# Low parts first in every second pair of pieces, in the gates, the convolution's output and the block's output projection

## What is computed

```
h = h + (p[i] @ pl_w_up[i]) * jax.nn.sigmoid(h @ pl_w_gate[i])           # plgate

proj = hn @ w_in
u, gb_in, gc_in, v_in, ga_lin, gbr_lin = jnp.split(proj, splits, axis=-1)
y_b = (gb_in * causal_depthwise_conv(gc_in * v_in, conv_w)) @ conv_out_w  # cout
gates = jax.nn.sigmoid(jnp.concatenate([ga_lin, gbr_lin], axis=-1) + b_gate)   # ga, gbr
g_a, g_b = jnp.split(gates, 2, axis=-1)
h = h + (g_a * y_a + g_b * y_b) @ w_o                                     # wo
```

## Time and profile before

| what | value |
|---|---|
| median of 3 runs | 2665.52 us (2665.11 to 2665.89) |
| the profiled execution | 2665.68 us |
| its span, first to last instruction | 2663.6 us |
| mean granted TensorE clock | 0.999 |
| PE busy | 2652.8 us, 15711 matmuls |
| DVE busy | 1658.5 us, 62% |
| ACT busy | 1236.0 us, 46% |
| DMA | 502.92 MB, mean 189 GB/s |

### The profile page before, as it was taken

The page is one execution under the profiler, slowest core; times in us unless marked ns, Lnnn a source line. Parts: engine busy times, 40 slices in busy tenths (PEclk is TensorE's granted clock), DMA queues, the critical chain, the costliest instruction groups (busy, mean ns, idle before and its releaser), DMA issues.

```text
span 2663.6 us, 39872 instructions
## 1 busy us (share of the span) xinstructions
PE 2652.8 (100%) x15711; PEld 2347.5 (88%) x15711; DVE 1658.5 (62%) x1645; ACT 1236.0 (46%) x1355; POOL 0.8 (0%) x7
## 2 busy tenths in 40 slices
PE   9999999999999999999999999999999999999998
PEld 8889888888888888888999999888888888888887
DVE  6567766555565556795676666556765645564555
ACT  5456554444444444565443443444554434443444
POOL 0000000000000000000000000000000000000000
PEclk9999999999999999999999999999999999999999
DMA  8554555655656555555555555555565555565553
GB/s 291 184 174 145 195 189 193 193 193 188 198 181 205 181 199 189 185 191 191 176 175 189 181 184 182 190 182 190 189 205 189 189 189 189 189 198 192 180 192 138
DMA packets 254251, 502.92 MB, mean 189 GB/s; under 512 B 8130, under 2 KB 11652, under 8 KB 253988
## 3 DMA queue, kind: packets, MB, share of 16 engines
q1 hardware_dynamic: 252180, 497.61, 56.6%
q10 hardware_dynamic: 1952, 3.68, 0.4%
HBM read 498.37 MB, written 2.88 MB: 188 GB/s over the span
## 4 chain that ended last, share of the span: by engine, by line
PE 99%; DVE 0%; ACT 0%; DMA 0%; issue 0%; ACTq 0%; DVEq 0%
PE ps L1359 49%; PE ps L1373 24%; PE ps L1392 4%; PE ps L1394 4%; PE ps L1393 4%; PE ps L1412 4%; PE ps L1411 4%; PE ps L1410 3%; PE ps L1403 0%; PE ps L1402 0%; PE ps L1404 0%; PE ps L1322 0%; DMA xtok<-in_x_dram 0%; PE ps L1547 0%; PE ps L1545 0%; PE ps L1546 0%
## 5 line engine op out<-in xcount | busy, mean ns | idle before, releaser
L825 DVE TENSOR_TENSOR lo<-raw,hi 128x1024 fp32r<-128x1024 f32 x940 | 1127.8, 1223 | 852.2 <-ACT hi L491 843.6
L491 ACT ACTIVATE hi<-raw 128x1024 fp32r<-128x1024 f32 x940 | 971.5, 1055 | 1061.2 <-PE ps L1373 483.6
L1359 PE MATMUL ps<-A,hi 128*128 128x512 f32 x3648 | 862.8, 393 | 0.0
L1359 PEld LDWEIGHTS ps<-A,hi 128*128 128x128 f32 x3648 | 675.6, 188 | 140.4
L1359 PE MATMUL ps<-B,hi 128*128 128x512 f32 x1984 | 477.5, 394 | 0.0
L1373 PEld LDWEIGHTS ps<-A,lo 128*128 128x128 f32 x3648 | 438.0, 188 | 12.0
L1373 PE MATMUL ps<-A,lo 128*128 128x256 f32 x3648 | 439.9, 277 | 0.0
L1359 PEld LDWEIGHTS ps<-B,hi 128*128 128x128 f32 x1984 | 365.3, 188 | 74.8
L1373 PEld LDWEIGHTS ps<-B,lo 128*128 128x128 f32 x1984 | 246.1, 188 | 10.0
L1373 PE MATMUL ps<-B,lo 128*128 128x256 f32 x1984 | 247.8, 279 | 0.0
L1412 PE MATMUL ps<-B,lo 128*128 128x258 f32 (+1 forms) x768 | 219.4, 286 | 0.0
(11 more groups left out here) (240 smaller groups left out, 1342.6 us busy)
## 6 DMA issues: line engine op xcount, KB each, us to landing
raw<-in_w_in_dram SPq DMA_DIRECT2D x136, 1024.0 KB, 5.1
raw<-in_ffn_w_dram SPq DMA_DIRECT2D x132, 1024.0 KB, 5.1
raw<-in_w_gate_up_dram SPq DMA_DIRECT2D x88, 1024.0 KB, 5.0
raw<-in_w_down_dram SPq DMA_DIRECT2D x44, 1024.0 KB, 5.1
raw<-in_w_out_dram SPq DMA_DIRECT2D x16, 1024.0 KB, 5.2
raw<-in_pl_w_gate_dram SPq DMA_DIRECT2D x16, 1024.0 KB, 5.1
raw<-in_conv_out_w_dram SPq DMA_DIRECT2D x16, 1024.0 KB, 5.1
raw<-in_w_o_dram SPq DMA_DIRECT2D x16, 1024.0 KB, 5.1
```

The source lines that it names most:

```text
L491: act.activation(hi[:, slot % RING], raw[:, raw_slot, 2 * (slot % 2):2 * (slot % 2) + 2, :], ACT.Copy).then_inc(hi_ready, 1)
L825: dve.tensor_tensor(lo[:, slot % RING], raw[:, slot // 2 % RAWS, 2 * (slot % 2):2 * (slot % 2) + 2, :], hi[:, slot % RING], ALU.subtract). ...
L1359: last = pe.matmul(ps[:, b0 + m, :], high(slot, kk, m), both, start=j == 0 and kk == 0, stop=ends and j == seg.pieces - 1 and kk == 1)
```

## The change

Five segments are added to the set: plgate, ga, gbr, cout and wo, all of two turns with two groups of eight pieces. What is computed stays the same but for the order in which products are added.

```
-SNAKED = {"qk", "out"} | {f"f{i}_{part}{c}" for i in (1, 2) for part in ("up", "down") for c in range(3)}
+SNAKED = {"qk", "out", "plgate", "ga", "gbr", "cout", "wo"} | {f"f{i}_{part}{c}" for i in (1, 2) for part in ("up", "down") for c in range(3)}
```

## The result

The changed kernel takes 2669.23 us (median of 18 runs, 2666.32 to 2670.94) against 2665.43 us (18 runs of the kernel before, 2665.07 to 2666.12). The ratio is 1.0013, 95% interval 1.0007 to 1.0019: slower by 3.8 us, forecast 4.2, and too little to be called a change at the 0.2% that I set. The changed kernel's runs lie 4.6 us apart, those before 1.1; that turns out to have a cause of its own. The profiled execution took 2668.11 us.

What follows compares the result with a forecast made beforehand. TensorE bounds the kernel at 99% of the chain, so only matmul pace and new waits count. Waits for late lo, less gains in pace, sum to +4.2 us: 2669.7 against the median, range 2664.5 to 2675.2, own range 2667.7 to 2673.5.

Steps and rivals of the forecast that it cites:

- Two paces, set by the block's length: PE's matmuls: blocks of 32 fall into 21.92 us per group of eight, blocks of 16 into 22.48; gain 10.2 us.
- the 0.43 for its long start: gbr's start: entered at the long pace, it pays 0.43 us until it is short, leaving a gain of 1.73.
- Late lo: Swapped pairs want lo up to 3.7 us sooner; PE waits where DVE makes it late, about 12 waits, longest 2.6 us.
- E: Start of a group on PE, when the last group's evacuation is released; lo times are counted from it.
- I take 15.72, since no row shows which pace follows a wait: Rest of a group after the second pair's second lo: 15.53 us at the short pace, 15.92 at the long.
- I grant no relief from slots that come free earlier: plgate's third and fourth groups: DVE's chain hangs on the group's start, not PE's later progress; +1.22 us each.
- -0.6 forecast: wo's last three groups: late lo at 6.43 us after the group's start, 22.29 us a group, together -0.6.
- The rival of absorbed waits: lo of swapped pairs come 1.3 to 2.7 us sooner than counted, slots freeing 0.9 sooner: -9.8, 2655.7 us; chance 0.12.
- ga's first group, with its read of B: The fourth pair reads B's last quarter, written slightly late, leaving 0.05 of the 0.41 us gain; -0.12 with the single pieces.
- up to 0.15 us on a restart: Upper bound: 0.15 us more at each of 12 PE waits, if a restart costs as after the sumsq matmuls; total +8.0.

Runs made afterwards that it cites:

- e7: The kernel before the change with no segment swapped at all, so blocks of 16 there too: 2696.85 us, ratio 1.0117.
- e6: Against the kernel before: all five segments as single pieces, 8 high and 8 low parts, none swapped: 2656.11 us, ratio 0.9965.
- e1: Only gbr, cout and wo swapped, plgate and ga as in the kernel before: 2660.51 us against 2665.49, ratio 0.9981.
- e4: The whole change, but the second pair of ga's second group keeps its high parts first: 2663.99 us, ratio 0.9996 to the kernel before.
- e8: The whole change with the reduce of plgate's second sum of squares on DVE left out: 2663.88 us, ratio 0.9994 to the kernel before.
- e9: Against the kernel before: plgate, ga, gbr, cout, pool and f1_down2 as single pieces of 8 and 8, wo swapped: 2654.85 us, ratio 0.9960.

## Why the prediction was right, and where it was not

**Two paces, set by the block's length**: right in the segments that the change touches, and shown (e7, e6, e1); not the whole rule, as plup shows. gbr came out at 88.11 us as worked out, with the 0.43 for its long start.

**Late lo**: right in place. In plgate I had the low parts of the first group's second pair at E + 8.01 and of the second group's fourth pair at 18.52 + 0.14; they started at 7.94 and 18.50. ga's was counted at E + 9.19 and came at 9.15. e4 and e6 show by removal, e8 by shortening, that these waits are the loss.

**"I take 15.72, since no row shows which pace follows a wait"**: mis-sized. Nine groups had this term. In the profile only the one with the clock's fall is followed by the long pace, the other eight need 15.53, 0.2 us less each; once in e1 it was the long one.

**"I grant no relief from slots that come free earlier"**: the step that failed: in wo's last three groups each late lo came 0.9 us sooner than counted. The last pair of a swapped group frees its first slot earlier, so DVE makes the next lo before the group's end instead of after it. In wo the evacuation's first step doesn't need the new accumulators and can start at once. DVE in wo's second group, first before the change (E = 1857.89), then in the changed kernel (E = 1862.32):

```profile
1858.30 1.23 DVE L825 TENSOR_TENSOR lo<-raw,hi 128x1024 fp32r<-128x1024 f32 x1 [3.26 <-ACT hi L491]
```

```profile
1861.83 1.23 DVE L825 TENSOR_TENSOR lo<-raw,hi 128x1024 fp32r<-128x1024 f32 x1 [2.18 <-ACT hi L491]
1862.98 1.22 DVE L880 TENSOR_TENSOR h<-h,r_fin 128x1024 f32<-128x1024 f32 x1
...
1866.63 1.22 DVE L825 TENSOR_TENSOR lo<-raw,hi 128x1024 fp32r<-128x1024 f32 x1
```

The lo before the evacuation started at E + 0.41 before and starts at E - 0.49 now, 0.9 us sooner. The late lo is done at E + 5.53, where the earlier trace rows gave 6.43; the wait is gone, and wo's last three groups are 21.92 us each, -1.7 for the -0.6 forecast. In plgate and ga the step behind is the copy from PSUM, which hangs on E, so there it brought 0.3 us a group at most: the waits of plgate's third and fourth group ended at E + 17.58 and 17.56 where I had 17.93, and 0.09 of that is the start 0.05 behind the lo in place of 0.14. The rival of absorbed waits had named the 0.9 us; it held in wo, and was far too small for plgate and ga. ga's first group, with its read of B, took 22.95 us, against 23.30 before and 23.18 forecast.

**The clock**: missing from the sum. I had put up to 0.15 us on a restart; a fall cost 1.6 and 1.9 us in the two profiles that have one, and does not come in every execution. Without it the profile's sum is +0.5 us (2668.11 - 2665.68 - 1.9), and the lowest runs stand at +0.9, both well under my +4.2. So that the median agrees with the forecast is in good part luck: two errors of opposite sign met, the relief and the short pace (over 3 us too dear), and the clock (some 3 us too cheap over the runs).

## What to carry to other kernels

Before an order is swapped for pace, find for every consumer when its input is ready and how much in hand it has, group by group: here one pair in eighty cost as much as three segments brought. Where a gain comes from a block's length, try the other lengths too, since one may have the same pace with a later need. And count a wait of TensorE like the 1.9 and 2.4 us here with the chance of a clock fall behind it: here it showed as clusters of run times, and not in a profile that happened to miss it.

## What the runs showed that I had not expected

- The same wait of TensorE, 2.43 and 2.44 us at one place in two executions, was followed once by a granted clock of 0.50 (1.2 GHz) with a loss of 1.9 us, once by 1.00. The wait of 1.89 in plgate was at full clock in the changed kernel's profile and followed by a fall in e4's. In e1, whose waits on a lo are at most 0.3 us, 11 runs lie within 0.7 us.
- Matmuls of 512 columns are spaced 229.0 or 233.4 ns, those of 256 columns 113.4 or 117.6, and in groups of six or eight pieces the block's length decides: 8 and 32 lead to the short spacing, 16 to the long one. plup, with blocks of 8 in groups of one piece, stays at the long one. Over the whole kernel e7 and e9 are 42 us apart, 1.6%, by the order of the matmuls. Why blocks of 16 differ stays open, and why plup does; no experiment here tried lengths of 4, 24 or 48.
- A matmul that had waited for a lo started 0.05 us after the lo's end.
